# Moving the transposes of a new X ahead of the last weight chunk of the stage that makes it

## What is computed

```
# first block
x = x + 0.5 * swiglu(rmsnorm(x), w_gate, w_up, w_down)          # f1
h = rmsnorm(x); proj = h @ w_in                                 # mixer: gMLP + stick-breaking attention
x = x + (g_a * (y_a @ w_branch_a) + g_b * (y_b @ w_branch_b)) @ w_out
x = x + 0.5 * swiglu(rmsnorm(x), w_gate2, w_up2, w_down2)       # f2
x = rmsnorm(x, final_norm)
# second block
x = layer_norm(ALPHA * x + gla_mixer(x))                        # gla
x = layer_norm(ALPHA * x + swiglu_ffn(x))                       # f3
x = layer_norm(ALPHA * x + moba_mixer(x, positions))            # moba
x = layer_norm(ALPHA * x + swiglu_ffn(x))                       # f4
```

## Time and profile before

| | |
|---|---|
| median of 3 runs | 1342.15 us (1342.01 to 1342.4) |
| the profiled execution | 1340.61 us, its span 1338.9 us |
| mean granted TensorE clock | 0.982 |
| busy: PE, DVE, ACT, POOL | 96%, 57%, 45%, 4% of the span |
| DMA | 50% of 16 engines for the weights |
| chain that ended last | PE 92%, DVE 4%, ACT 1%, POOL 1% |

### The profile page before, as it was taken

The page is one execution under the profiler, slowest core; times in us unless marked ns, Lnnn a source line. Parts: engine busy times, 40 slices in busy tenths (PEclk is TensorE's granted clock), DMA queues, the critical chain, the costliest instruction groups (busy, mean ns, idle before and its releaser), DMA issues.

```text
span 1338.9 us, 15419 instructions
## 1 busy us (share of the span) xinstructions
PE 1280.0 (96%) x6000; PEld 1042.0 (78%) x6000; DVE 765.9 (57%) x1027; ACT 608.1 (45%) x807; POOL 49.7 (4%) x111
## 2 busy tenths in 40 slices
PE   7999999999999999999989987999997998899997
PEld 6888887888887778888867655888885886788886
DVE  6755556656666655555446545555545767455554
ACT  5444435456656354444345333444434453343441
POOL 2000002000000000000000011000001000000000
PEclk9999999999999999999999988999997999899999
DMA  8665646654445455655364334655554544556551
GB/s 287 188 200 174 204 133 222 206 171 127 129 135 185 148 183 184 201 172 205 115 195 141 111 112 155 205 189 189 185 161 134 181 144 124 188 174 195 181 181 55
DMA packets 119752, 226.55 MB, mean 169 GB/s; under 512 B 8049, under 2 KB 16241, under 8 KB 119681
## 3 DMA queue, kind: packets, MB, share of 16 engines
q1 hardware_dynamic: 116976, 216.10, 50.0%
q0 software_dynamic: 2560, 8.95, 2.5%
q10 hardware_dynamic: 144, 0.52, 0.1%
HBM read 224.50 MB, written 1.05 MB: 168 GB/s over the span
## 4 chain that ended last, share of the span: by engine, by line
PE 92%; DVE 4%; ACT 1%; POOL 1%; issue 1%; DMA 1%; DVEq 0%; SPq 0%; POOLq 0%; ACTq 0%
PE ps L387 28%; PE ps L395 28%; PE ps L390 27%; PE ps L351 4%; DVE wl L1346 2%; PE ps L545 1%; PE ps L559 1%; DVE X L1424 1%; DMA raw<-in_ff_w_gate_dram 1%; POOL st L2060 1%; PE ps L692 1%; PE ps L694 1%; POOL st L2059 0%; DVE st L1410 0%; DVE X L1429 0%
## 5 line engine op out<-in xcount | busy, mean ns | idle before, releaser
L1346 DVE TENSOR_TENSOR wl<-raw,wh 128x1024 fp32r<-128x1024 f32 x409 | 487.1, 1218 | 250.2 <-ACT wh L836 246.3
L836 ACT ACTIVATE wh<-raw 128x1024 fp32r<-128x1024 f32 x409 | 422.3, 1054 | 231.1 <-PE ps L395 212.7
L387 PE MATMUL ps<-wh,XTH 128*128 128x512 f32 (+1 forms) x1184 | 456.9, 389 | 16.1 <-ACT XTH L869 16.1
L390 PE MATMUL ps<-wl,XTH 128*128 128x512 f32 (+1 forms) x1184 | 447.2, 381 | 0.0
L395 PE MATMUL ps<-wh,XTL 128*128 128x512 f32 (+1 forms) x1184 | 351.2, 383 | 21.8 <-DVE XTL L1384 21.8
L387 PEld LDWEIGHTS ps<-wh,XTH 128*128 128x128 f32 x1184 | 224.8, 190 | 65.0 <-issue 18.3
L395 PEld LDWEIGHTS ps<-wh,XTL 128*128 128x128 f32 x1184 | 218.1, 190 | 66.6 <-DVE XTL L1384 24.2
L390 PEld LDWEIGHTS ps<-wl,XTH 128*128 128x128 f32 x1184 | 225.1, 190 | 40.1 <-issue 0.5
L390 PE MATMUL ps<-wl,HHf 128*128 128x512 f32 x352 | 140.1, 398 | 0.0
L387 PE MATMUL ps<-wh,HHf 128*128 128x512 f32 x352 | 138.8, 394 | 0.0
L395 PE MATMUL ps<-wh,HLf 128*128 128x512 f32 x352 | 110.7, 395 | 0.0
(11 more groups left out here) (269 smaller groups left out, 989.9 us busy)
## 6 DMA issues: line engine op xcount, KB each, us to landing
raw<-in_ffn_w_gu_dram SPq DMA_DIRECT2D x88, 512.0 KB, 4.5
raw<-in_w_in_dram SPq DMA_DIRECT2D x56, 512.0 KB, 3.8
raw<-in_ff_w_gate_dram SPq DMA_DIRECT2D x44, 512.0 KB, 4.2
raw<-in_ff_w_up_dram SPq DMA_DIRECT2D x44, 512.0 KB, 4.6
raw<-in_ff_w_down_dram SPq DMA_DIRECT2D x44, 512.0 KB, 3.6
raw<-in_ffn_w_down_dram SPq DMA_DIRECT2D x44, 512.0 KB, 4.3
raw<-in_gla_w_in_dram SPq DMA_DIRECT2D x24, 512.0 KB, 3.8
raw<-in_moba_w_in_dram SPq DMA_DIRECT2D x24, 512.0 KB, 4.2
```

Of the source, the lines that this page charges most:

```text
L387: e.matmul(o, lh[:, kt, rows(t)], wh[:, s, w], start=kt == 0, stop=False)
L390: e.matmul(o, lh[:, kt, rows(t)], wl[:, s, w], start=False, stop=False)
L836: e.activation(wh[:, j % NS, 0:m], raw[:, j % NR, 0:m], ACT.Copy).then_inc(S("wh"), 1)
L1346: e.tensor_tensor(wl[:, j % NS, 0:m], raw[:, j % NR, 0:m], wh[:, j % NS, 0:m].bitcast(F32), ALU.subtract).then_inc(S("wl"), 1)
```

## The change

Two tables say which halves are turned in the last block of the old stage (`FIRST`) and which in the first block of the new one (`LAST`).

```diff
-        LATE = [(0, 1), (1, 1)]
         EARLY = [(0, 0), (1, 0)]
+        FIRST = {2: [(0, 1)], 3: [(0, 1)], 4: ROWS[:2], 5: ROWS[:2], 6: ROWS[:2], 7: ROWS[:2]}
+        LAST = {2: [(1, 1)], 3: [(1, 1)], 4: ROWS[2:], 5: ROWS[2:], 6: ROWS[2:], 7: ROWS[2:]}
...
         def pe_first(e, name, stage, halves):
             for now in pe_gemm(e, name, XTH, XTL, wait_x(stage), 4):
-                if len(halves) == 4 and now == (0, 0):
-                    turn(1)
-                elif now == (0, 2):
-                    turn(1)
-                elif now == (0, 3):
-                    turn(len(left))
+                if now == (0, 3):
+                    for t, h in halves:
+                        pe_turn_x(e, stage, t, h)
+
+        def pe_last(e, name, lh, ll, stage, wait=None, tail=4):
+            b, at, end, width, kts = blocks[name]
+            for now in pe_gemm(e, name, lh, ll, wait, tail):
+                if now == (1, end - at - 1) and stage in FIRST:
+                    for t, h in FIRST[stage]:
+                        pe_turn_x(e, stage, t, h)
+                yield now
...
-            for now in pe_gemm(e, f"{f}d1", HH, HL, None, 5):
+            for now in pe_last(e, f"{f}d1", HH, HL, stage + 1, None, 5):
...
-                turn_o(1)
...
-            pe_plain(e, "go0", GTH, GTL, wait_parts(lambda t, half: ("o", t, half)), 4)
-            pe_plain(e, "go1", GTH, GTL, None, 4)
+            for now in pe_gemm(e, "go0", GTH, GTL, wait_parts(lambda t, half: ("o", t, half)), 4):
+                if now == (0, 2):
+                    turn_o(1)
+            for _ in pe_last(e, "go1", GTH, GTL, 5):
+                pass
...
 # ACT: the squares of one half at a time
-            def squares_row(t, *updated):
+            def squares(t, half, *updated):
...
+            def first_x(stage):
+                for r, h in FIRST.get(stage, ()):
+                    split_x(stage, r, h)
...
                 for t in block(f"{f}d1", 5):
                     if t is None:
+                        if steps == 0 and f in ("f1", "f2"):
+                            for r in range(2):
+                                squares(r, 0, *ev(f"{f}d0", r))
...
+                    if t == 1:
+                        first_x(stage + 1)
+                    if f in ("f1", "f2"):
+                        squares(t, 1, *ev(f"{f}d1", t))
...
 # DVE, in the last block of each stage: row tile 0's low parts ahead of row tile 1's residual
+                    if t == 1:
+                        first_x(stage + 1)
+                    down(1, t)
...
+                        if half == 0 and t == 0:
+                            low_o(1)
+                        if half == 1 and t == 1:
+                            first_x(5)
                         if t is not None:
                             residual(f"go{half}", t, half, 5)
```

More of the change, by code:

```diff
@@ L599, in pe_mixer @@
                     turn_m(1)
-            for now in pe_gemm(e, "wo1", YAH, YAL, None, 4):
+            for now in pe_last(e, "wo1", YAH, YAL, 3):
                 if now == (0, 3):
@@ L618, in pe_gla, with turn_o @@
             ins.then_inc(S("used"), 1)
+            def turn_o(half):
+                for t in range(2):
+                    e.wait_ge(S("oo"), 2 * half + t + 1)
+                    pe_turn(e, ("o", t, half), [O[:, t, half * 512 + i * P:half * 512 + (i + 1) * P]
+                                                for i in range(4)])
             def gates():
@@ L801, in pe_moba @@
                         advance(side)
-            pe_plain(e, "mo1", OTH, OTL, None, 4, side)
+            for now in pe_last(e, "mo1", OTH, OTL, 7):
+                if now is None:
+                    advance(side)
             while side:
@@ L873, in split_x, with ffn @@
                 split(key, XTH[:, hsl(half), rows(t)], aux4(key))
-            def squares_row(t, *updated):
[L877 to L887, removed]
+            def squares(t, half, *updated):
+                e.wait_ge(*updated)
+                if at_chunk["squares"] is not None:
+                    e.wait_ge(*at_chunk["squares"])
+                at_chunk["rows"] += half
+                ins = e.activation(SQ, X[:, t, cols(half)], ACT.Square, accum_out=ss[:, 2 * t + half:2 * t + half + 1])
+                if half == 0:
+                    at_chunk["squares"] = (S("act"), own(ins))
+                else:
+                    ins.then_inc(S("sq"), 1)
+                    at_chunk["squares"] = (S("sq"), at_chunk["rows"])
             def tables(name):
                 e.preload_act_table_set(name)
-            def ffn(f, stage, halves, rs_stage, side, behind_d0=None):
+            def first_x(stage):
+                for r, h in FIRST.get(stage, ()):
+                    split_x(stage, r, h)
+            def ffn(f, stage, halves, rs_stage, side):
                 HH, HL, SG, HB = ffn_tiles[f]
@@ L1127, in gla, with split_o @@
                 high_to(blocks["low"][1] - 1 + LEAD)
+                def split_o(half):
+                    for t in range(2):
+                        key = ("o", t, half)
+                        split(key, GTH[:, hsl(half), rows(t)], aux4(key))
                 def gates():
@@ L1180, in head_out @@
                                          accum_out=OS[:, i, 0:1]).then_inc(S("osq"), 1)
-                    def split_o(half):
-                        for t in range(2):
-                            key = ("o", t, half)
-                            split(key, GTH[:, hsl(half), rows(t)], aux4(key))
                     for h in range(5):
@@ L1306, in moba @@
                     advance(side)
-                no_readout("mo1", 4, side)
+                for t in block("mo1", 4):
+                    if t is None:
+                        advance(side)
+                    elif t == 1:
+                        first_x(7)
                 while side:
@@ L1777, in gla, with low_o @@
                 e.tensor_copy(lowT[:, :], ps[0:16, bank_of("low", 0), 0:256]).then_inc(ev("low", 0)[0], 1)
+                def low_o(half):
+                    for t in range(2):
+                        key = ("o", t, half)
+                        low(key, GTL[:, hsl(half), rows(t)], aux4(key), GTH[:, hsl(half), rows(t)])
                 def gates():
@@ L1850, in half_out @@
                                             ALU.mult).then_inc(S("oo"), 1)
-                    def low_o(half):
-                        for t in range(2):
-                            key = ("o", t, half)
-                            low(key, GTL[:, hsl(half), rows(t)], aux4(key), GTH[:, hsl(half), rows(t)])
                     for h in range(5):
```

83 lines of the change are left out of this document (43 added, 40 removed).

## The result

The changed kernel takes 1303.38 us (median of 4 runs, 1302.37 to 1304.62) against 1342.08 beside it (1340.58 to 1342.4): a ratio of 0.9714, with a 95% interval of 0.9697 to 0.9731. The profiled execution took 1302.37 us, its span is 1300.7.

What follows compares the result with a forecast made beforehand. PE bounds the kernel between seams, so time is won only at seams: 32.8 + 4.7 + 0.7 + 2.6 = 40.8 us off 1340.6 gives 1299.8, 1301.3 as median, stated as 1302; range 1297 to 1312.

Steps and rivals of the forecast that it cites:

- Seams 4 to 7: Starts of the t=1 pass at these four seams: 6.0, 8.3, 10.2 and 8.3 us won, together 32.8 us.
- The formula: Seams 4 to 7: the t=1 pass starts 5.1 us after the old last norm step of row 1, 1.3 from DVE's queue.
- The GLA output: Turning O's second half behind the first two chunks of go0 wins 4.7 us.
- Seams 2 and 3: Seam 2 wins 2.6 but keeps 0.7 us, the rest lost through POOL and the group norm; seam 3 wins 2.6.
- At the start: Row (1,0) turned one chunk later at the kernel's start: costs nothing while two chunks cover it, otherwise under 0.6 us.
- The step that failed: From the first chunk of the t=1 pass on, both kernels run alike; no loss was counted in gla.
- Rival A: Clock falls again at seams 4 to 7: at most 2.4 us in four places, 9.6, giving 1311 us; chance 0.16.
- Rival B: DVE bounds further at four seams, both casts and row 1's low part needed first: 5 to 10 us; chance 0.09.
- Rival C: Weight loads bound the whole kernel without the waits: nothing won, or slower, 1373 us at 165 GB/s; chance 0.03.
- Rival D: Nothing moves: the turn ahead of the last chunk only shifts the stop to its other side; chance 0.02.
- The table load: ACT at seams 2 and 3: 1.28 us in the trace; with the skill page's draining, their terms shrink 2.8 us together.

Runs made afterwards that it cites:

- low_gap: The changed kernel with DVE's low part of (0,1) moved at seams 4 to 7 from ahead of row 1's residual into its norm; 1298.29 us, ratio 0.9684.
- delay: The changed kernel with row 1's statistics computed again inside its norm, once, three and six times at seams 5, 6 and 7; 1311.98 us, ratio 0.9779.
- u_go: The changed kernel with the second half of gla's O turned ahead of the first chunk of go0, as before; 1306.44 us, ratio 0.9747.
- pool_fix: The changed kernel with POOL's wait for gmlp_w_s and its memset behind the first half of the group norm's roots; 1300.82 us, ratio 0.97.
- u_s4: The changed kernel with seam 4 alone as before the change; 1306.54 us, ratio 0.9741.
- gbc_late: The changed kernel with POOL's load of gla_norm_g issued after those of wgk and bgk and behind both LA; 1301.44 us, ratio 0.9704.
- u_s5: The changed kernel with seam 5 alone as before, all four halves of X turned in f3's first block; 1307.81 us, ratio 0.9757.
- best: Changed kernel, gla_norm_g loaded behind LA, gmlp loads earlier, POOL's gmlp_w_s wait later, (0,1)'s low part in row 1's norm, (1,0) turned as before at start; 1295.83 us.
- after_again: The changed kernel itself, unedited, timed once more beside the variants; 1304.5 us, ratio 0.9728.
- dec_late: The changed kernel with PE's 16 tiny matmuls on LA in gla one weight chunk later, loads unmoved; 1302.25 us, ratio 0.9716.

## Why the prediction was right, and where it was off

**The time.** 1302 was said, 1303.4 came, 1304.5 in the second set. Against the profiled execution, for which the sum was made, 1299.8 stands against 1302.37: 2.6 us too little, 2.15 of them in gla. The range held.

**Seams 4 to 7.** Right, step by step: 6.0, 8.3, 10.2 and 8.3 were worked out, 6.16, 8.35, 10.22 and 8.33 came. The last norm step of row 1 to the t=1 pass takes 3.86 us (3.8 said). The formula rested on DVE's queue, and `low_gap` and `delay` show that this is the bound in both directions. One part was sized otherwise: PE stops for 1.3 us, not 1.5 to 2 (or "some 3", as the prediction has it in another place), and for the cast for 0.24, not 0.5.

**The GLA output.** 4.7 said, 4.76 measured, 4.83 given back by `u_go`.

**Seams 2 and 3.** At seam 2, 2.6 won and 1.9 given back were said; 2.52 and 2.13 came, through the chain that was named, POOL to the group norm to the sixth cast, as `pool_fix` shows. PE's wait for that cast is 1.62 us (1.6 said). What the text did not see is that POOL's late root was no necessity: moving two of its instructions removes it. At seam 3, 2.6 said, 2.49 measured. At the start no loss was counted, and −0.29 came; but the same position lies between 37.39 and 38.85 us in profiles of kernels with the same program up to there, so this says nothing of the edit.

**The step that failed** is the premise that from the t=1 pass on both kernels run alike; gla stands in the sum with no loss for that reason. I had followed PE beyond the pass at seam 2 alone. Behind seam 4 there is the same kind of place: loads of POOL (gla_norm_g, wgk, bgk) stand beside the weight chunks and don't scale with PE's gain. That costs 2.15 us in gla, and `u_s4` and `gbc_late` show both its cause and that it can be had back. The clock is the larger part: two profiles with little or no clock loss there, `u_s5` and `low_gap`, lost only 0.4 and 0.7 us. The range held all the same, since 2.15 us are little against the 38 won.

**Rival A, the clock**, was right in kind and too dear: not 2.4 us at each seam but 1.6, and not always. It goes with the median lying above the first profile (that execution had a mean clock of 0.997, the other three 0.996), and it had a chance of 0.16 as an event that happens or doesn't, when it is one that happens in some executions at some seams.

**Rival B** fell: one cast, not two, stands between the norm and the t=1 pass. **Rival C** fell as a bound of the whole, since the kernel now moves 174 GB/s, as it needs to; but in a small place it was right, in gla, where loads that come together did delay work. **Rival D** fell: row 0 was ready when PE came to it (a wait of 0.29 us at seam 5).

**The table load and the clock.** The Trainium skill's page ScalarE: Activation LUTs (What ACT_TABLE_LOAD costs) adds some 1.38 us of draining. In the changed kernel the table load at seam 2 starts at 203.96, where the instruction ahead ends (203.76 + 0.19), and lasts 1.28, and the cast behind it starts at 205.25; there is no such gap, and seams 2 and 3 won 2.5 us each as the rows had it. The Trainium skill's page TensorE: Matmul & The Clock Gate (A second HAM failure mode) names a clock that swings when short idle gaps stand, often enough, between groups of matmuls. The trace agrees in part: the clock does fall without a long stop, but here behind one wait of 1.3 us rather than many. At that wait it fell in 6 of 26 passes, at 2.07 us and more (`delay`) each of three times, and at 0.6 and less at the seams (`low_gap`, `best`) in none of six. The length of the wait alone doesn't decide: before the change, PE waited 2.3 us at seams 2 and 3, and the clock from 200 to 660 us was 1.00.

## What to carry to other kernels

When a seam is shortened, follow PE not only to where the gain is made but on to the next place where something with its own clock is waited for: a load that another engine issues, a root that POOL computes, a sum that DVE owes. Each such thing that doesn't move takes some of the gain back, and often only because an instruction that nobody needs yet stands ahead of one that somebody does. And look at the shortest waits that remain: going from 1.3 to 0.6 us at the seams was worth more than the difference, since the clock then stayed up (0.998 to 0.999 in all four executions of `low_gap`). The times still varied there by 2.4 us; they stopped varying, to 0.8 us, in `best`, where gla no longer lost its clock either.

## What the runs showed of the hardware

- The granted clock can fall to half behind a single wait of 1.3 us, and the same program does it in one execution and not in the next: seam 6, 1.00 against 0.66 over 5 us, 1.6 us of time. It did so in 6 of 26 passes over seams 5 to 7, and behind the wait for a cast at seam 2 (1.3 to 1.8 us) in one profile of nine. None of six passes with waits of 0.6 us or less fell; six are few against that rate, and the stronger sign is the mean clock of all nine executions of these two kernels, 0.998 or 0.999.
- It can fall with hardly any wait: in gla it fell in six of the eight profiles in which `LA` was ready less than 0.2 us ahead of the sixteen tiny matmuls (128x2 outputs, 1.9 to 2.0 us in all) or behind PE. In four of the six PE had waited for it for 0.25 to 0.49 us, in `after_again` and `delay` no wait is on record. It did not fall in `u_s5` (ready 0.14 us ahead) and `low_gap` (a wait of 0.42). Where `LA` was ready 0.6 us ahead or more (before, `gbc_late`, `dec_late`, `u_s4`, `best`) it never did. What decides between the cases isn't settled.
- One load of 512 KB by POOL (gla_norm_g), issued beside weight chunks of 512 KB and ahead of two small loads, kept ACT waiting for 6.08 us; with it the chunks' median landing from 668 to 700 us was 8.8 us, without it (`gbc_late`) 5.2. Issued behind both `LA`, some 26 us later, it cost nothing. The kernel before had it in the same place with a median of 4.8 us and no loss, so the loss needs both the load and a PE that comes 6 us earlier.
